# Gate units in five places of a mixing chunk instead of eight

## The reference

```
xn = rmsnorm(x, g_mix)
mq, mk, mv, mo, mi, mf, aq, ak, av, gt = split(xn @ w_in)
h_m, C, n, m = mlstm(mq, mk, mv, li, lf, C0, n0, m0, chunk)       # chunk by chunk
h_m = h_m * rsqrt(mean(h_m^2) + EPS) * g_mhead * sigmoid(mo)
h_a = swa_attend(rope(aq), rope(ak), av, ..., sinks)
ga, gb = split(sigmoid(gt))
x = x + (ga * (h_m @ w_a) + gb * (h_a @ w_b)) @ w_out
x = rmsnorm(x + conv_ffn(rmsnorm(x, g_ffn)), g_final)
```

## Time and profile before

| | |
|---|---|
| median of three runs | 3063.32 us |
| the profiled execution, its own time | 3068.29 us |
| its span | 3066.3 us |
| TensorE busy | 2922.9 us, 95% |
| VectorE busy | 1783.8 us, 58% |
| ScalarE busy | 1390.4 us, 45% |
| GpSimd busy | 649.2 us, 21% |
| gate matmuls L599 | 2400 in all, 800 of each kind |

### The profile page before, as it was taken

One profiled execution on the slowest core, in us unless ns is written; L12 is line 12 of the kernel. 1 busy time (PEld: TensorE's weight loads), 2 busy tenths in 40 slices (PEclk: granted clock), 3 DMA queues, 4 the chain that ended last, 5 costly groups with the idle time before them and its releaser, 6 DMA issues.

```text
span 3066.3 us, 43381 instructions
## 1 busy us (share of the span) xinstructions
PE 2922.9 (95%) x16129; PEld 2770.4 (90%) x16129; DVE 1783.8 (58%) x2653; ACT 1390.4 (45%) x2432; POOL 649.2 (21%) x940
## 2 busy tenths in 40 slices
PE   5999969899999968999999999999999999999997
PEld 4888858888888968899999999999999999999996
DVE  3222146667766634765558755687646775477654
ACT  2222134545544423554446543465435555355443
POOL 1111011011111112211224211242112422124222
PEclk9999979999999989999999999999999999999998
DMA  4333265445454436344343453444443444333433
GB/s 139 116 104 104 71 195 187 146 147 169 146 168 137 144 114 201 101 163 128 117 144 125 153 165 121 138 139 147 156 142 128 141 144 146 122 117 119 138 116 78
DMA packets 242803, 419.67 MB, mean 137 GB/s; under 512 B 38563, under 2 KB 155683, under 8 KB 242595
## 3 DMA queue, kind: packets, MB, share of 16 engines
q1 hardware_dynamic: 240482, 416.77, 42.7%
q10 hardware_dynamic: 2112, 0.13, 0.0%
HBM read 352.12 MB, written 65.74 MB: 136 GB/s over the span
## 4 chain that ended last, share of the span: by engine, by line
PE 59%; DVE 1%; SPq 1%; issue 1%; DMA 1%; ACT 1%; POOL 0%; POOLq 0%; DVEq 0%; ACTq 0%
PE f_ps L1596 39%; PE f_ps L1601 19%; DMA f_sgi<-gate_rows 0%; PE f_st L1608 0%; SPq L1552 0%; SPq L1556 0%; SPq L1528 0%; DVE f_rinv L1808 0%; DMA f_raw<-in_w_out 0%; DVE f_ml L1803 0%; DVE f_xres L1812 0%; SPq L1510 0%; POOL f_sgi L1952 0%; DVE f_wl L1787 0%; ACT f_mh L1682 0%
## 5 line engine op out<-in xcount | busy, mean ns | idle before, releaser
L1787 DVE TENSOR_TENSOR f_wl<-f_raw,f_wh 128x1024 fp32r<-128x1024 f32 (+2 forms) x460 | 540.4, 1175 | 160.8 <-ACT f_wh L1652 154.9
L1596 PE MATMUL f_ps<-f_xh,f_wh 128*128 128x416 f32 x1760 | 617.9, 351 | 4.4 <-DVE f_xl L1821 4.3
L1596 PE MATMUL f_ps<-f_xl,f_wh 128*128 128x416 f32 x1760 | 618.6, 352 | 0.0
L1652 ACT ACTIVATE f_wh<-f_raw 128x1024 fp32r<-128x1024 f32 (+2 forms) x460 | 442.4, 964 | 292.5 <-PE f_ps L1601 274.6
L1601 PE MATMUL f_ps<-f_xh,f_wl 128*128 128x416 f32 x1760 | 367.6, 350 | 0.0
L1596 PEld LDWEIGHTS f_ps<-f_xh,f_wh 128*128 128x128 f32 x1760 | 330.0, 188 | 11.1 <-DVE f_xl L1821 6.7
L599 PE MATMUL pp<-gxh,gwh 128*128 128x416 f32 x800 | 303.5, 379 | 35.9 <-DVE gxl L576 35.9
L1596 PEld LDWEIGHTS f_ps<-f_xl,f_wh 128*128 128x128 f32 x1760 | 330.8, 188 | 3.9 <-issue 0.6
L1601 PEld LDWEIGHTS f_ps<-f_xh,f_wl 128*128 128x128 f32 x1760 | 329.9, 188 | 2.3
L1840 DVE SCALAR_TENSOR_TENSOR f_c<-f_u,f_taps,f_c 128x416 f32<-128x416 f32 (+2 forms) x264 | 154.3, 598 | 297.3 <-ACT f_c L1704 297.1
L1596 PE MATMUL f_ps<-f_gh,f_wh 128*128 128x416 f32 x880 | 310.9, 353 | 5.9 <-issue 5.9
(11 more groups left out here) (239 smaller groups left out, 5032.8 us busy)
## 6 DMA issues: line engine op xcount, KB each, us to landing
f_raw<-in_w_up SPq DMA_DIRECT2D x220, 512.0 KB, 3.6
f_raw<-in_w_dn SPq DMA_DIRECT2D x120, 384.0 KB, 3.0
graw<-in_w_gate SPq DMA_DIRECT2D x80, 512.0 KB, 4.0
gate_rows<-gsgo SPq DMA_DIRECT2D x100, 208.0 KB, 2.7
f_raw<-in_w_br SPq DMA_DIRECT2D x40, 512.0 KB, 3.8
f_raw<-in_w_out SPq DMA_DIRECT2D x40, 512.0 KB, 3.5
f_sgi<-gate_rows SPq DMA_DIRECT2D x80, 208.0 KB, 3.8
proj_rows<-a_out SPq DMA_DIRECT2D x17, 900.0 KB, 3.6
```

Source lines behind the costliest of these rows:

```text
L1596: pe.matmul(ps[n][:, 0:TB], wh[s][:, (col + k) * P:(col + k) * P + P], x[:, k0 + k, :], start=(k == 0 and x is xhi), stop=False)
L1652: act.activation(wh[v % WS][:, 0:w], raw[s][:, 0:w], ACT.Copy).then_inc(ev("w_hi"), 1)
L1787: dve.tensor_tensor(wl[n][:, 0:w], raw[s][:, 0:w], wh[n][:, 0:w].bitcast(F32), ALU.subtract).then_inc(ev("w_lo"), 1)
```

## The change

The eight places of gate halves in a chunk become five, with (2, 3, 2, 2, 2) halves instead of (1, 2, 1, 1, 1, 2, 1, 2); both add to 11. Steps of the two branches that had gate halves between them now stand next to each other, and on TensorE and ScalarE the next chunk's transposes come ahead of those of hm. The functions themselves, the halves ahead of chunk 1 and in the samples' chunk are the same.

```diff
--- before.py
+++ after.py
@@ -303,7 +303,7 @@
 SGN = MO + 2 * KT
 GUNITS = SPANS * SGN
 GRAWS, GWS = 3, 3
-SLOTS = (1, 2, 1, 1, 1, 2, 1, 2)
+SLOTS = (2, 3, 2, 2, 2)
 EARLY, LATE = 6, 6
 
 
@@ -1161,24 +1161,21 @@
             mix_pe_a(pe, n, q)
             units_pe(pe, n, 0)
             mix_pe_scores(pe, n, q, 1)
+            mix_pe_last(pe, n, q)
             units_pe(pe, n, 1)
-            mix_pe_last(pe, n, q)
-            units_pe(pe, n, 2)
             mix_pe_ptr(pe, n, q, 0)
             mix_pe_str(pe, n, q)
             mix_pe_inter(pe, n, q)
-            units_pe(pe, n, 3)
+            units_pe(pe, n, 2)
             mix_pe_pv(pe, n, q, 0)
             mix_pe_intra(pe, n, q)
-            units_pe(pe, n, 4)
             mix_pe_ptr(pe, n, q, 1)
             mix_pe_cup(pe, n, q)
-            units_pe(pe, n, 5)
+            units_pe(pe, n, 3)
             mix_pe_pv(pe, n, q, 1)
-            units_pe(pe, n, 6)
+            mix_pe_tr(pe, n + 1, 1 - q)
             mix_pe_hm(pe, n, q)
-            mix_pe_tr(pe, n + 1, 1 - q)
-            units_pe(pe, n, 7)
+            units_pe(pe, n, 4)
         mix_pe_s(pe, N, 0)
         mix_pe_a(pe, N, 0)
         samp_pe_kc(pe)
@@ -1228,25 +1225,21 @@
             mix_dve_sm(dve, n, q, 1)
             mix_dve_pn(dve, n, q, 0)
             mix_dve_s(dve, n, q)
-            units_dve(dve, n, 1)
             mix_dve_last(dve, n, q)
             mix_dve_isc(dve, n, q)
+            units_dve(dve, n, 1)
             mix_dve_inter(dve, n, q)
+            mix_dve_pn(dve, n, q, 1)
             units_dve(dve, n, 2)
-            mix_dve_pn(dve, n, q, 1)
-            units_dve(dve, n, 3)
             mix_dve_h(dve, n, q)
-            units_dve(dve, n, 4)
             rotate(dve, n + 1, 1 - q)
             mix_dve_c(dve, n, q)
-            units_dve(dve, n, 5)
+            units_dve(dve, n, 3)
             mix_dve_h2(dve, n, q)
             if n < CHUNKS:
                 mix_dve_a(dve, n + 1, 1 - q)
             mix_dve_h3(dve, n, q)
-            units_dve(dve, n, 6)
-            units_dve(dve, n, 7)
-
+            units_dve(dve, n, 4)
         dve.wait_ge(ev("m_out"), 16)
         dve.memset(m0[:], 0.0).then_inc(ev("m0_clear"), 1)
         mix_dve_a(dve, N, 0)
@@ -1282,24 +1275,21 @@
         for n in range(1, CHUNKS + 1):
             q = (n - 1) % 2
             mix_act_p(act, n, q, 0)
+            mix_act_dx(act, n, q)
             units_act(act, n, 0)
-            mix_act_dx(act, n, q)
-            units_act(act, n, 1)
             mix_act_p(act, n, q, 1)
             mix_act_w(act, n, q)
-            units_act(act, n, 2)
+            units_act(act, n, 1)
             mix_act_pt(act, n, q, 0)
             mix_act_st(act, n, q)
+            units_act(act, n, 2)
+            mix_act_ha(act, n, q, 0)
+            mix_act_pt(act, n, q, 1)
             units_act(act, n, 3)
-            mix_act_ha(act, n, q, 0)
+            mix_act_ha(act, n, q, 1)
+            mix_act_tr(act, n + 1, 1 - q)
+            mix_act_hm(act, n, q)
             units_act(act, n, 4)
-            mix_act_pt(act, n, q, 1)
-            units_act(act, n, 5)
-            mix_act_ha(act, n, q, 1)
-            units_act(act, n, 6)
-            mix_act_hm(act, n, q)
-            mix_act_tr(act, n + 1, 1 - q)
-            units_act(act, n, 7)
         mix_act_dx(act, N, 0)
         samp_act_kc(act)
         units_act(act, N, 0)
```

## The result

The changed kernel takes 3091.32 us in the median of four runs (3089.42 to 3092.92), against 3064.37 for the kernel before beside it; the ratio is 1.0084 with an interval of 1.0070 to 1.0099. It is slower: the two medians are 27.0 us apart, the ratio gives some 26. The profiled execution has a span of 3090.5 us, 24.2 more than before.

A forecast was written before the change was run, and what follows sets the result against it. TensorE's instruction stream bounds the kernel; even chunks 6.9, chunk 16 1.7, odd chunks 14.1, chunk 7 5.5 and chunk 4 -2.2 sum to +26 us, profiled 3094.3, less 5.0 gives 3089. Likeliest case 3079 to 3099; wider range 3073 to 3107.

The forecast's parts named there:

- part 2: Front of the chunk, up to L730: nothing charged; up to 1 us in 8 chunks if VectorE's 4.1 is short.
- part 1: Switches between instructions at the three removed places: 0.1 us per chunk gained, chunk without waits 37.5 us.
- The rival beside which I named the Trainium skill: Fewer places save tiling-mode switches on TensorE: three pairs a chunk, 27 us off, 3062, no change; 4%.
- part 3: Back of the chunk, L730 to hm: with less cover, hm waits 1.8 us in even and 2.1 in odd chunks.
- TensorE's path: From L730 to hm without waits, TensorE takes 9.15 us, the four transposes of aq included.
- The wait at hm: Sign in the profile: TensorE waits for VectorE at L773 1 to 2 us in nearly all 16 chunks, more in odd.
- Contention: In hm's chain GpSimd delays VectorE in each chunk: second rotation product takes 1.33 us, 128x4 scaling 0.69.
- The rival priced at 1.3 x 16 = 21 us: GpSimd and VectorE do not meet in hm's chain: 21 us off, 3068; 5%, partial forms (3070 to 3079) another 5%.
- part 4: TensorE's waits for a new xl: chunk 4 waits 4.5 us (-3.4), chunks 11 and 15 wait as before.
- Chunk 7: Eight span splits of 4.10 us push hm's chain by 3.6: +4.7, up to 2 more if clock falls; taken +5.5.
- Chunk 15: Same span-start wait as before, 4.0 us, plus the odd chunk's 2.0.
- The clock at hm: New waits at hm drop the clock to 1.2 GHz: 3121 if in every chunk, 3095 to 3105 in a few; 10%.

The follow-up runs named there:

- the front alone: Kernel before with places of 1, 3, 1, 1, 2, 1, 2 halves and L693 directly behind the second scores, back as before: 3065.05 us, ratio 0.9997.
- a half put back: Changed kernel with one gate half moved from its third place to between the second L765 and the next chunk's transposes: 3063.59 us, ratio to before 0.9994.
- hm first: Changed kernel with hm's transposes ahead of the next chunk's again, on TensorE and ScalarE: 3119.8 us, one run.
- the back alone: Changed kernel with the chunk's front as in the kernel before, places of 1, 2, 1, 3, 2, 2 halves: 3094.3 us, one run.
- the split late: Changed kernel with VectorE's weight split of the fourth place put behind hm instead of ahead of the mean square: 3072.2 us, one run.

## Why the prediction was right, point by point

- *The front is covered* (part 2): right. Apart from the span starts no wait stands ahead of L730 in the changed kernel, and the front alone made no difference.
- *The seams* (part 1): I took a gain of 0.1 us a chunk; there is none. L730 stands 23.14 us into the chunk (742.66 - 719.52), 4.56 later than before, for two halves that I had at 4.5. In the back two steps in a row even cost some: L752 comes 1.00 behind L730, where a gate half stood 0.92 behind it before, and L740 comes 1.10 behind L752 instead of 0.97. The rival beside which I named the Trainium skill (TensorEngine Tiling (Array Packing), Key Properties) falls: the switches are as many as before, as counted, and no time is saved.
- *The chain* (part 3): right. It ends 11.10 us behind L730 in even chunks (752.87 + 0.89 - 742.66), where I had 10.92, since the last multiplication took 0.89 instead of 0.69; in odd ones 11.30 (792.48 + 0.89 - 782.07), where I had 11.2. The chunks came to 39.41 and 39.62; forecast were 39.3 to 39.4 and 39.6. The cost is 1.22 and 2.01 us a chunk against 1.15 and 2.0.
- *TensorE's path* from L730 to hm was longer than my 9.15 us. From L730 to the second L765 it takes 7.42 us (750.08 - 742.66), and from there to hm, in the run with a half put back, where nothing waits, 4.38, of which a half is 2.37: together 9.4. So the time lost ahead of hm is 11.15 - 9.4 = 1.7 us in even and 11.35 - 9.4 = 1.9 in odd chunks, where my sum had 1.8 and 2.1. The error in the path and the 0.1 of the seams work against those in the chain and partly cancel, so a hit to 0.1 us is better than the terms were.
- *The wait at hm* is listed as 1.05 and 1.49, below these. As said ahead, part of it is taken by L664 and L669, which now wait for aq and, in even chunks, for ScalarE's copy; another part is the time in which weights are loaded.
- *Contention*: the 1.33 us come back in each chunk, the 0.68 in even chunks only, not in each as the prediction said. The square on ScalarE gives the first its price, 0.84 us, where I had 0.85 to 0.9. That the two engines get in each other's way here is what the Trainium skill's sentence on the shared interfaces (GPSIMD Engine Reference, Key points) leads one to expect; that sentence has no price. The rival priced at 1.3 x 16 = 21 us was too dear: in odd chunks the gate bank's emptying sets the chain, so the first pair alone is worth 0.84 in half of the chunks, 6 us in all (3085.05 in one run).
- *The span starts* (part 4): chunk 4 waits 4.30 (forecast 4.5), chunk 7 2.25 (about 2), chunk 15 3.99 (4.0).
- *Chunk 7* lost 5.31 us, near the 5.5, but not as I had it. The eight splits took 5.13 us instead of 4.10: GpSimd's additions for `aq` ran beside the first two, and each of these took 1.1 us, against 0.58 for each of the six behind them. This contention was in none of my terms. hm's chain came 4.5 late, not 3.6. The clock did fall, behind the 2.25 of the span start and not at hm. That held TensorE up ahead of hm, so that hm waited 1.63 and L664 some 0.6, where I had 3 or more, and cost nothing further. That my allowance for the clock covers the longer splits is luck.

```profile
704.68 1.76 POOL L654 TENSOR_TENSOR aq<-rc,rs 128x256 f32<-128x256 f32 x2
704.78 5.13 DVE L576 TENSOR_TENSOR gxl<-gxs,gxh 128x416 fp32r<-128x416 f32 x8
```

- *Chunk 15* lost 1.13 instead of 2.0 with the same wait. The clock explains it. Before, it was at 0.50 for all of the 5.2 us behind the wait; after, it came back sooner, and the same stretch has a mean of 0.67, which is 5.2 x (0.67 - 0.50) = 0.9 us of full-rate work more. I had taken the slow stretch as unchanged. Before and then after:

```profile
985.10:990.30 5.20, 5.20 (x16) 4.46 (x18) 4.51 (x8) 1.78 (x8) 0.00 (x0) 0.50 0.00 0
```

```profile
1007.50:1012.70 5.20, 5.20 (x19) 5.04 (x20) 4.50 (x8) 1.78 (x8) 0.00 (x0) 0.67 0.00 0
```

- *The clock at hm*, a rival with 10%, did not come at 1.0 to 1.6 us. With hm first it came at 2.6 to 2.8 in 6 of 14 chunks, so the rival was real, and the swap kept it away.

The sum was 26.0 against 24.3 in the profiled executions, 1.7 too high. Too much was charged for chunk 15 (0.9), chunk 3 (0.6: the kernel before had its 0.57 for pt there), chunk 16 (0.5), chunk 4 (0.3) and chunk 7 (0.2); too little for the even chunks (0.07 each) and chunk 11 (0.4). From the sum to the time one more step was off: the profiled execution before stood 5.0 us above its median, and I took the same off after, where it stands 1.2 above (3092.5 to 3091.32). The 1.7 too much and the 3.8 too little leave the forecast of 3089 some 2 us under the 3091.32; that it is so near is in part luck.

## What to carry to other kernels

Work put between two steps of a chain is cover for the chain that ends at the next of them: before joining places, measure from the last step that feeds the chain to the one that waits for it, on both engines, and keep the filler on that stretch. The place joined here that was not on such a stretch cost nothing and brought nothing. Where the engine that sets the time waits in few spots, as at the four span starts here, a second buffer filled in another engine's idle time was worth about five times the best reordering (19.6 us, 3062.42 - 3042.85, against the 3.9 by which the swap alone stood below the kernel before beside it).

## What the runs showed of the hardware

- A 128x320 product of two float32 tiles on VectorE took 0.48 us alone and 1.33 beside GpSimd's square of 128x512, in every chunk of the changed kernel; with the square on ScalarE it took 0.48 in every chunk. A 128x4 scaling took 0.68 in even chunks, where GpSimd's additions for `aq` ran until its end, and 0.17 in odd ones.
- TensorE's granted clock is no simple matter of the length of a wait. In the chunks of the ten kernels it stayed at 1.00 behind all waits up to 1.99 us (chunk 7's hm, the back alone). Between 2 and 3.2 us it went both ways: it fell to 0.50 behind 2.25 in chunk 7 of the changed kernel and behind 2.61 in chunk 6 with hm first, and stayed at 1.00 behind 2.64 in chunk 10 with hm first, behind 3.03 in chunk 11 with the split late and behind 3.20 in chunk 7 with a half back. Behind the waits of 3.5 us and more it was at 0.50 every time.
- Eight 128x128 transposes behind a 129-column matmul group start 1.00 us behind its start, against 0.92 for a gate matmul there (L752 and L599 behind L730, after and before).
